# Hybrid attention encoder on one core: dilated products a step later, distance tables on two engines, value loads inside the blocks, four transposed pieces ahead of the layer barrier

## The chip, the cores and the metric

The kernel runs on one core of one Trainium2 chip. The time is device microseconds of one execution; a kernel is timed in several executions and the median is given. PE is the matrix engine (TensorE), DVE the vector engine, ACT the scalar engine, POOL GpSimd, and SP the engine whose queue issues the DMA transfers.

## The reference, cut to what matters

Two layers, a sequence of 1024 tokens, width 1024, everything in fp32. A layer projects the normalised input to queries, keys and values of three groups of heads, mixes each group in its own way, normalises, projects back and adds, and then does a SwiGLU feed-forward.

```
for l in range(DEPTH):                      # DEPTH = 2
    h = rms_norm(x, attn_norm[l])
    x = x + hybrid_mixer(h, ...)            # A: 2-D neighbourhood, 4 heads; B: +-128 tokens, 6 heads;
    h = rms_norm(x, ffn_norm[l])            # C: dilated windows, 6 heads
    x = x + swiglu(h, w_gu[l], w_down[l])

for window, d in ((128, 1), (512, 4), (2048, 16)):      # group C
    # every d-th token forms a sub-sequence of s // d tokens
    o, lse = banded_attention(to_sub(q), to_sub(k), to_sub(v), window // (2 * d), slopes, d)
# the three results are weighted by softmax(lse) over the branches and added
# banded_attention: sc = q @ k.T * hd**-0.5 - slope * distance * d, masked; softmax; @ v
```

## The kernel before

Everything is written out by hand: each engine has a program, and they meet at semaphores. A layer is one such set of programs, closed by a barrier of all engines. In a layer come the value projections, the query and key projections with their norms (units `UR`/`UH`/`UL`), the attention, the output projection, and the feed-forward (`RAW`, `WH`, `WL`, `OPH`, `ABH`, `ABL`), whose products are split into high and low fp32r parts.

The attention is a pipeline of steps k = 0 to 57 over 224 score tiles, four tiles to a step. A tile is one head of one block of 128 queries. The first 96 tiles (steps 0 to 23) are dilated: 16 groups of 6 heads, groups 0 to 7 of branch d=16 ("c3", 128 keys) and 8 to 15 of branch d=4 ("c2", 192 scores of 256 keys). From tile 96 on (step 24) follow eight token blocks of 16 tiles (6 of group B, 6 of branch d=1, 4 of group A), four steps each. In step k:

- PE computes the scores of tiles 4k to 4k+3 (line 2373, `psum<-KS,QS` or `psum<-QK`), then the weighted sums with the values of tiles 4k-8 to 4k-5 (`weigh`, line 2482, `psum<-VR,PT`), then transposes the probabilities of tiles 4k-4 to 4k-1 (line 2439, `psum<-ident,T`).
- DVE adds the distance table to the scores and takes the minimum (`tmin`, line 1659, `T<-TC,psum`), four tiles, and then copies the transposed probabilities from PSUM to `PT` (line 1830), up to step 12 all of them, later one of two pieces; ACT copies the other (line 1241).
- ACT takes the exponentials (line 1219), stores each finished group of sums to its buffer `G` (line 1212), and in steps 2 to 19 makes one distance table per step (`distance_table`, line 1151): the six of `TC2`, the six of `TC1`, the six of `TB`.
- POOL gathers the strided queries and keys of a dilated group into `QS` and `KS` (lines 2172 and 2173), one group per 1.5 steps, two buffers.
- SP's queue stores each dilated group to DRAM (`store_group`, lines 936 and 939; four `G` buffers, and `tmin` of group g waits until group g-4 is out), then loads the values of group g+4 to `VR` (`load_values`, lines 904 to 908), and from group 8 on also the bias tables and the values of the token blocks: nine loads to `VC` (line 952) and eight to `VA` (line 956). Behind all of them stands the load that brings the two dilated results back for token block 0 (line 986); DVE's `branch_min` (line 1746) in step 27 waits for it, `branch_min` of a later block for its own.

At the end of layer 0, PE transposes the first two of the sixteen pieces of the next layer's input (`turned`, line 2320, `psum<-ident,XN`) ahead of the barrier, and behind it multiplies piece 0 (`value_half(0, 0)`, line 2307, `psum<-VWH,HH`) and transposes pieces 2, 3 and 4 before it can go on with piece 1. Pieces 2 and 3 use banks whose last sums DVE adds to `X` just ahead (`add_last`, line 2098).

Of the kernel before, what the change touches and what calls it, by code (L numbers as in the profile page):

```python
# [22 lines left out]
def build_program(nc, x, gains, w_in, rpb, w_out, w_gu, w_down, out):  # L23
# [43 lines left out]
    with ctx:  # L67
# [96 lines left out]
        QS = sb("QS", [P, 2, 3, P], F32, "Q", 2048)  # L164

# [54 lines left out]
        WARM_START, WARM_LAYER = 72, 8  # L220
# [86 lines left out]
        for l in range(depth):  # L307
          with ExitStack() as layer:
# [38 lines left out]
            g_out_s = [sem(f"g_out{i}") for i in range(4)]  # L347
# [12 lines left out]
            dist_signed, dist_abs, dist_made = sem("dist_signed"), sem("dist_abs"), sem("dist_made")  # L360
            row_made, col_made, mask_made = sem("row_made"), sem("col_made"), sem("mask_made")
# [157 lines left out]
            order = []  # L519
            n_pt = 0  # L520
# [138 lines left out]

            def group_buf(bd, s):  # L660

                if bd["kind"] in ("c3", "c2"):
                    return G4[:, s // 6, :], s % 6
                return (GB[:, :], s) if s < 6 else (GC[:, 0, :], s - 6) if s < 12 else (GA, s - 12)
# [147 lines left out]
            def _(sp):  # L812
# [40 lines left out]
                sp.wait_ge(dist_made, 1)  # L853
# [76 lines left out]
                def store_group(gi):  # L930
                    sp.wait_ge(grp_s, gi + 1)
                    slot = gi % 4
                    if gi < 8:
                        g16 = g_dil[1].rearrange("(j r) c -> r j c", r=16)
                        for rr in range(2):
                            sp.dma_start(g16[2 * gi + rr], G4[64 * rr:64 * rr + 64, slot, :]).then_inc(g_out_s[slot], 16)
                    else:
                        g4 = g_dil[0].rearrange("(t p r) c -> r t p c", p=P, r=4)
                        sp.dma_start(g4[(gi - 8) // 2, gi % 2], G4[:, slot, :]).then_inc(g_out_s[slot], 16)

                for gi in range(4):
                    load_values(gi)

# [10 lines left out]
                def load_grid(c):  # L954

                    sp.dma_start(VA[ROWS * c:ROWS * c + ROWS, :, :, :].rearrange("p m h d -> p m (h d)"),
                                 v_a.rearrange("(r m c) d -> c r m d", m=MT, c=COLS)[c]).then_inc(va_in, 16)
# [3 lines left out]
                for gi in range(C_GROUPS):  # L961
# [18 lines left out]
                for slot in range(4):  # L980
                    sp.wait_ge(g_out_s[slot], 16 * 6)
# [1746 lines left out]
```

## Time and profile before

| | |
|---|---|
| median of 3 executions | 2338.93 us (2336.89 to 2340.94) |
| the profiled execution | 2340.14 us, of which its span is 2338.4 us |
| instructions | 40610 |
| PE busy | 2282.7 us |
| DVE, ACT, POOL busy | 1598.8, 1068.1 and 657.7 us |
| DMA | 225.34 MB, 96 GB/s on average |

A row of a view of instructions has the start in us from the span's start, the duration, engine, line, operation, output<-inputs, form and count; in brackets how long the engine had been idle before it, and what ended that. The lines are those of the kernel before; in the diff and the changed kernel they are a few higher.

### The profile page before, as it was taken

How to read it: one execution, taken by the hardware profiler on the slowest of the kernel's cores; microseconds unless marked ns; L12 is line 12 of the kernel's file. 1: busy time of each engine (PE TensorE's matmuls, PEld its weight loads, DVE VectorE, ACT ScalarE, POOL GpSimd, SP SyncE). 2: the span in 40 equal slices, each digit the busy share in tenths (PEclk: the TensorE clock that was granted, in tenths of full speed). 3: DMA queues.
4: the chain of work that ended last, by engine and by line, in shares of the span. 5: the costliest groups of instructions: out<-in, count | busy, mean ns of one | idle time of the engine just before them, and what ended most of it. 6: DMA issues, size and time to landing. Idle time of an engine off the chain costs nothing. (4 is left out here: it accounts for less than half of the span.)

```text
span 2338.4 us, 40610 instructions
## 1 busy us (share of the span) xinstructions
PE 2282.7 (98%) x15504; PEld 1889.8 (81%) x15504; DVE 1598.8 (68%) x2895; ACT 1068.1 (46%) x2048; POOL 657.7 (28%) x571
## 2 busy tenths in 40 slices
PE   9999889999999999999999998999999999999999
PEld 9988766787888888888899887667878888888887
DVE  5389879738555555789844897796475555557898
ACT  4333789735322222443443337896452223224434
POOL 1000456311444444100010005562124444440000
PEclk9999999999999999999999999999999999999999
DMA  7231341232222211721452314303322222218223
GB/s 249 66 53 53 95 119 31 101 124 70 81 82 90 82 55 55 291 82 54 137 175 58 56 45 117 105 28 123 104 72 82 81 81 83 62 45 315 68 81 104
DMA packets 234028, 225.34 MB, mean 96 GB/s; under 512 B 50292, under 2 KB 192116, under 8 KB 233848
## 3 DMA queue, kind: packets, MB, share of 16 engines
q1 hardware_dynamic: 233848, 222.89, 30.2%
q8 instruction: 119, 1.95, 0.3%
q14 instruction: 61, 0.50, 0.1%
HBM read 171.00 MB, written 53.41 MB: 96 GB/s over the span
## 5 line engine op out<-in xcount | busy, mean ns | idle before, releaser
L1925 DVE TENSOR_TENSOR WL<-RAW,WH 128x512 fp32r<-128x512 f32 x132 | 160.6, 1218 | 151.3 <-ACT WH L1374 151.3
L2677 PE MATMUL psum<-ABH 128*128 128x512 f32 x616 | 240.1, 390 | 1.1 <-DVE X L2008 1.1
L2678 PE MATMUL psum<-ABL,ABH 128*128 128x512 f32 x616 | 239.7, 389 | 0.0
L2679 PE MATMUL psum<-ABH,ABL 128*128 128x512 f32 x616 | 239.7, 389 | 0.0
L2643 PE MATMUL psum<-HL,WH 128*128 128x512 f32 x704 | 217.4, 390 | 0.7 <-DVE HL L1931 0.7
L2643 PE MATMUL psum<-OPH_t,WH 128*128 128x512 f32 x528 | 205.9, 390 | 3.5 <-DVE U L1946 3.5
L2643 PE MATMUL psum<-OPL_t,WH 128*128 128x512 f32 x528 | 205.7, 390 | 1.0 <-DVE OPH_t L1931 1.0
L1925 DVE TENSOR_TENSOR WL<-WS,WH 128x512 fp32r<-128x512 f32 x172 | 138.6, 807 | 84.2 <-ACT WH L1374 84.2
L2275 POOL TENSOR_TENSOR WS<-RAW 128x512 f32<-128x512 f32 x84 | 143.3, 1706 | 131.0 <-DMA x_res<-X 131.0
L2307 PE MATMUL psum<-HH,UH 128*128 128x512 f32 x448 | 174.5, 389 | 0.0
L2309 PE MATMUL psum<-HH,UL 128*128 128x512 f32 x448 | 174.3, 389 | 0.0
L2308 PE MATMUL psum<-HL,UH 128*128 128x512 f32 x448 | 174.3, 389 | 0.0
L1612 DVE RECIPROCAL RM<-RM 128x512 f32<-128x512 f32 x52 | 174.0, 3346 | 0.0
L1219 ACT ACTIVATE T<-T,G 128x192 f32<-128x192 f32 (+3 forms) x352 | 152.9, 470 | 17.1 <-DVE G L1659 15.7
L2643 PEld LDWEIGHTS psum<-HL,WH 128*128 128x128 f32 x704 | 131.7, 188 | 29.2 <-DVE HL L1931 1.5
L2172 POOL COPY QS<-QK 128x384 f32<-128x384 f32 x32 | 30.0, 937 | 438.4 <-DVE QK L1615 253.9
L2307 PE MATMUL psum<-PH,HH 128*128 128x512 f32 (+1 forms) x384 | 143.7, 374 | 0.0
L2309 PE MATMUL psum<-PH,HL 128*128 128x512 f32 (+1 forms) x384 | 142.6, 371 | 0.0
L2308 PE MATMUL psum<-PL,HH 128*128 128x512 f32 (+1 forms) x384 | 142.4, 371 | 0.0
L2643 PE MATMUL psum<-OPH_b,WH 128*128 128x512 f32 x352 | 137.3, 390 | 0.0
L2677 PEld LDWEIGHTS psum<-ABH 128*128 128x128 f32 x616 | 115.6, 188 | 26.5 <-DVE X L2008 2.0
L2643 PE MATMUL psum<-OPH_b,WL 128*128 128x512 f32 x352 | 137.0, 389 | 0.0
(270 smaller groups left out, 5526.2 us busy)
## 6 DMA issues: line engine op xcount, KB each, us to landing
RAW<-in_w_gu SPq DMA_DIRECT2D x176, 256.0 KB, 3.9
WDS<-in_w_down SPq DMA_DIRECT2D x88, 256.0 KB, 2.7
UR<-in_w_in SPq DMA_DIRECT2D x56, 256.0 KB, 3.3
g_mid<-GRES SPq DMA_DIRECT2D x28, 512.0 KB, 2.6
WDK<-in_w_down SPq DMA_DIRECT2D x44, 256.0 KB, 6.1
x_res<-X SPq DMA_DIRECT2D x2, 4096.0 KB, 13.3
PR<-in_w_out SPq DMA_DIRECT2D x32, 256.0 KB, 4.9
X<-x_res SPq DMA_DIRECT2D x2, 4096.0 KB, 13.7
```

Source lines behind the costliest of these rows:

```text
L1219: a.activation(T[:, t_slot(n), off:off + w], T[:, t_slot(n), off:off + w], ACT.Exp, scale=-1.0, bias=G[:, 6 * V1 + place_:6 * V1 + place_ ...
L1612: v.reciprocal(RM[:, hf, :], RM[:, hf, :]).then_inc(rec_s, 1)
L1925: v.tensor_tensor(WL[SLOT[i, j]][:, :, :], w_source(i, j), WH[SLOT[i, j]][:, :, :].bitcast(F32), ALU.subtract).then_inc(w_lo, 1)
L2172: g.tensor_copy(dst, dilated_rows(bd, T_CQ, q, P)).then_inc(staged, 1)
L2275: g.tensor_tensor(to[i][:, :, :], first, second, op).then_inc(w_sum, 1)
L2307: t.matmul(dst, sh, mh, start=start, stop=False)
L2308: t.matmul(dst, sh, ml, start=False, stop=False)
L2309: return t.matmul(dst, sl, mh, start=False, stop=stop)
L2643: last = t.matmul(dst[:, :], w[SLOT[i, j]][:, k, :], h[o][:, k, :], start=(i in (1, 5, 6) and k == 0 and part == 0), stop=(i in (2, 3, 4) ...
L2677: t.matmul(dst, ah, bh, start=open_, stop=False, skip_group_check=True)
L2678: t.matmul(dst, ah, bl, start=False, stop=False, skip_group_check=True)
L2679: last = t.matmul(dst, al, bh, start=False, stop=shut, skip_group_check=True)
```

## The change

Five edits, with their code below.

1. `weighed_at`: in the dilated steps the weighted sums are those of tiles 4k-12 to 4k-9, a step later than before. Step 25 does eight tiles, and from step 26 on all is as it was.
2. The dilated groups go round six buffers, not four: the four of `G4`, `GB`, and a new `GX`.
3. Of the 18 distance tables made in steps 2 to 19, ACT keeps those of steps 2, 4, 6, 8 and 10; DVE makes the other 13, behind its copies of the step.
4. Of the nine loads of `VC`, three stay among the dilated groups and six move between the token blocks; of each of the eight loads of `VA`, the half for blocks 0 to 3 stays and the half for blocks 4 to 7 moves behind the first load of the dilated results.
5. Four pieces, not two, are transposed ahead of the barrier, and four transposes of the identity follow them, whose result nothing reads.

Two pairs of setup semaphores are also merged into one each.

```diff
+            def weighed_at(k):
+                if k <= DILATED_STEPS:
+                    return range(max(4 * k - 12, 0), max(4 * k - 8, 0))
+                return range(4 * k - (12 if k == DILATED_STEPS + 1 else 8), 4 * k - 4)
...
+        G_DIL = [G4[:, 0, :], G4[:, 1, :], G4[:, 2, :], G4[:, 3, :], GB[:, :], GX[:, :]]
...
+            def group_slot(gi):
+                return gi % 6
+            def groups_out(slot, gi=C_GROUPS):
+                return sum(32 if before < 8 else 16 for before in range(slot, gi, 6))
...  # ACT, act_step
-                            if 2 <= k < 8:
+                            if k in (2, 4, 6):
                                 distance_table(TC2[:, k - 2, :], 384, 256, 4 * SLOPES[B_H + k - 2])
-                            elif 8 <= k < 14:
+                            elif k in (8, 10):
                                 distance_table(TC1[:, k - 8, :], 384, 256, SLOPES[B_H + k - 8])
-                            elif 14 <= k < 20:
-                                distance_table(TB[:, k - 14, :], 0, 384, SLOPES[B_ORDER[k - 14]])
...  # DVE, dve_step, behind copy_unit
+                def distance_table(tab, first, w, slope):
+                    v.tensor_scalar(tab, DIST[:, first:first + w], slope, None, ALU.mult).then_inc(table_s, 1)
+                    if k in (3, 5, 7):
+                        distance_table(TC2[:, k - 2, :], 384, 256, 4 * SLOPES[B_H + k - 2])
+                    elif k in (9, 11, 12, 13):
+                        distance_table(TC1[:, k - 8, :], 384, 256, SLOPES[B_H + k - 8])
+                    elif 14 <= k < 20:
+                        distance_table(TB[:, k - 14, :], 0, 384, SLOPES[B_ORDER[k - 14]])
...  # SP
-                        load_neighbours(2 * h)
-                        load_neighbours(2 * h + 1)
...
-                        if gi == C_GROUPS - COLS // 2:
-                            load_neighbours(MT)
-                        c = 2 * (gi - (C_GROUPS - COLS // 2))
-                        load_grid(c)
-                        load_grid(c + 1)
+                        m = gi - (C_GROUPS - COLS // 2)
+                        if m < NEAR_FIRST:
+                            load_neighbours(m)
+                        load_grid(2 * m, 0)
+                        load_grid(2 * m + 1, 0)
...
                 for b in range(MT):
...
                         sp.dma_start(GC[:, 1 + n, :], g_dil[n][b * P:b * P + P, :]).then_inc(g_back, 16)
+                    if b + NEAR_FIRST <= MT:
+                        sp.wait_ge(vc_in, 16 * (b + NEAR_FIRST))
+                        load_neighbours(b + NEAR_FIRST)
+                    if b == 0:
+                        sp.wait_ge(va_in, 16 * COLS)
+                        for c in range(COLS):
+                            load_grid(c, 1)
...  # PE, behind the barrier and ahead of it
-                    pe.sem_inc(xt_s, 2)
+                    pe.sem_inc(xt_s, 4)
...
-                for j in range(2 if l else 0, 4):
+                for j in range(4 if l else 0, 4):
                     turned(j)
...
-                    for j in range(2):
+                    for j in range(4):
+                        if j == 2:
+                            pe.wait_ge(last_added, 4)
                         turned(j)
+                    for i in range(WARM_LAYER):
+                        t.transpose(bank[2][:, P * i:P * i + P], ident[:, :], ident[:, :])
```

On PE the first weighted sums stand between the scores and the transposes of step 2. Before, from the scores of step 1 to those of step 3:

```order
L2431 MATMUL psum<-ident,T 128x128 x4
L2373 MATMUL psum<-KS,QS 128x128 x4
L2482 MATMUL psum<-VR,PT 64x65 x8
L2431 MATMUL psum<-ident,T 128x128 x4
L2373 MATMUL psum<-KS,QS 128x128 x4
L2482 MATMUL psum<-VR,PT 64x65 x8
L2439 MATMUL psum<-ident,T 128x64 x8
```

And now:

```order
L2464 MATMUL psum<-ident,T 128x128 x4
L2406 MATMUL psum<-KS,QS 128x128 x4
L2464 MATMUL psum<-ident,T 128x128 x4
L2406 MATMUL psum<-KS,QS 128x128 x4
L2516 MATMUL psum<-VR,PT 64x65 x8
L2472 MATMUL psum<-ident,T 128x64 x8
```

The order within a step (scores, sums, transposes) stays; one set of sums is gone from step 2. It comes back in step 25, where 16 rows of the last dilated sums become 32. Before, at steps 24 and 25:

```order
L2373 MATMUL psum<-QK 128x256 x4
L2482 MATMUL psum<-VR,PT 64x65 x16
L2439 MATMUL psum<-ident,T 128x64 x16
L2373 MATMUL psum<-QK 128x256 x2
L2373 MATMUL psum<-QK 128x192 x2
L2482 MATMUL psum<-VR,PT 64x65 x16
```

And now:

```order
L2406 MATMUL psum<-QK 128x256 x4
L2516 MATMUL psum<-VR,PT 64x65 x16
L2472 MATMUL psum<-ident,T 128x64 x16
L2406 MATMUL psum<-QK 128x256 x2
L2406 MATMUL psum<-QK 128x192 x2
L2516 MATMUL psum<-VR,PT 64x65 x32
```

On DVE a table stands between the copies of step 3 and the first `tmin` of step 4 (`ISA` is `tmin` and the reading of its minimum). Before:

```order
L1659 ISA G_96 128x1
L1830 COPY PT<-psum 128x256 x2
L1659 ISA T,G_96<-TC_89,psum 128x128
L1659 ISA G_96 128x1
L1659 ISA T,G_96<-TC_89,psum 128x128
```

And now:

```order
L1682 ISA G_96 128x1
L1853 COPY PT<-psum 128x256 x2
L1869 TENSOR_SCALAR TC_90<-DIST 128x256
L1682 ISA T,G_96<-TC_89,psum 128x128
L1682 ISA G_96 128x1
```

Whatever holds the table up holds up the next step's `tmin` too. On PE at the layer's end, before:

```order
L2679 MATMUL psum<-ABH,ABL 128x512
L2320 MATMUL psum<-ident,XN 128x128 x8
L2693 UNCONDITIONAL_BRANCH
L2301 UNCONDITIONAL_BRANCH
L2307 MATMUL psum<-VWH,HH 128x384
```

And now:

```order
L2712 MATMUL psum<-ABH,ABL 128x512
L2353 MATMUL psum<-ident,XN 128x128 x16
L2728 MATMUL psum<-ident 128x128 x4
L2730 UNCONDITIONAL_BRANCH
L2334 UNCONDITIONAL_BRANCH
L2340 MATMUL psum<-VWH,HH 128x384
```

Eight transposes moved ahead of the barrier (the first branch ends the layer's program), with four more behind them.

## Rows read from the trace of the kernel before

**Rows 1.** The page: busy time (share of the span) and instructions.

```profile
PE 2282.7 (98%) x15504; PEld 1889.8 (81%) x15504; DVE 1598.8 (68%) x2895; ACT 1068.1 (46%) x2048; POOL 657.7 (28%) x571
```

**Rows 2.** Busy time by stretch: us, then engines, clock share, DMA share, GB/s.

```profile
200.00:250.00 50.00, 50.00 (x222) 41.11 (x221) 45.91 (x31) 20.23 (x32) 0.00 (x0) 1.00 0.10 31
```

**Rows 3.** Timeline, one step of branch d=16 in layer 0.

```profile
263.45 0.71 PE L2482 MATMUL psum<-VR,PT 128*64 128x65 f32 x16 [0.39 <-DVE PT L1830]
264.10 0.46 PE L2439 MATMUL psum<-ident,T 64*128 64x64 f32 x8
264.59 0.76 DVE L1830 COPY PT<-psum 128x256 f32<-128x256 f32 x2 [0.41 <-PE psum L2439]
265.50 0.30 PE L2482 MATMUL psum<-VR,PT 128*64 128x65 f32 x3 [0.44 <-DVE PT L1830]
```

**Rows 4.** Busy by stretch (PE, PEld, DVE, ACT, POOL), dilated steps of both layers.

```profile
259.30:278.69 19.39, 15.29 (x289) 12.77 (x288) 14.26 (x92) 17.01 (x54) 15.10 (x16) 1.00 0.42 103
278.69:286.13 7.44, 6.65 (x128) 5.55 (x128) 5.42 (x29) 6.93 (x19) 4.97 (x5) 1.00 0.61 166
286.13:303.09 16.96, 14.32 (x282) 12.38 (x280) 9.02 (x46) 13.40 (x34) 9.24 (x8) 0.90 0.81 229
303.09:316.52 13.43, 12.53 (x278) 10.57 (x276) 9.20 (x47) 11.74 (x30) 8.40 (x11) 1.00 0.70 205
316.52:319.75 3.23, 2.70 (x56) 2.14 (x56) 2.01 (x11) 2.76 (x7) 3.15 (x4) 1.00 0.52 145
1423.84:1443.41 19.57, 16.15 (x304) 13.61 (x304) 14.36 (x92) 16.68 (x54) 15.84 (x16) 1.00 0.43 107
1443.41:1450.71 7.30, 6.28 (x115) 4.90 (x112) 5.34 (x28) 6.82 (x19) 4.23 (x4) 1.00 0.68 177
1450.71:1464.79 14.08, 12.51 (x282) 10.81 (x280) 9.11 (x47) 13.15 (x34) 9.25 (x8) 1.00 0.93 261
1464.79:1478.22 13.43, 12.53 (x278) 10.55 (x276) 9.20 (x47) 11.75 (x30) 7.18 (x9) 1.00 0.75 209
```

**Rows 5.** Timeline, the weighted sums of one step of branch d=4.

```profile
300.62 1.15 PE L2482 MATMUL psum<-VR,PT 128*64 128x65 f32 x32 [0.20 <-DVE PT L1830]
```

**Rows 6.** Timeline of PE, the longest stop in the dilated steps.

```profile
291.87 0.77 PE L2482 MATMUL psum<-VR,PT 128*64 128x65 f32 x18 [0.15 <-ACT PT L1241]
294.52 1.13 PE L2482 MATMUL psum<-VR,PT 128*64 128x65 f32 x14 [1.88 <-issue]
```

**Rows 7.** DVE operations by line: duration ns min/median/max, first and last start.

```profile
L1621 DVE TENSOR_TENSOR SQL<-SQ,SQH x56: 679/684/1326, 94.7 to 1418.8; 128x512 fp32r<-128x512 f32 x56
L1562 DVE TENSOR_SCALAR XN<-X,rstd x16: 746/753/756, 512.5 to 1698.8; 128x1024 f32<-128x1024 f32 x16
L1697 DVE TENSOR_SCALAR gvare<-gvar x48: 142/146/154, 332.6 to 1611.2; 128x1 f32<-128x1 f32 x48
```

**Rows 8.** SP's queue: timeline, then the loads of VR from issue to landing.

```profile
271.75 1.23 SPq L936 DMA_DIRECT2D g_d<-G  x2
273.03 1.24 SPq L904 DMA_DIRECT2D VR<-v_c  x2
...
DMA to landing us min/median/max: 2.3/2.7/5.6
```

**Rows 9.** Waits in step 27 of layer 1: us in total, times, longest.

```profile
DVE nmin L1746 <- DMA G<-g_d: 1.6, 1, 1.6
```

**Rows 10.** Timeline at the barrier between the layers.

```profile
1173.32 1.04 PE L2320 MATMUL psum<-ident,XN 128*128 128x128 f32 x8
1174.67 0.75 DVE L1542 SCALAR_TENSOR_TENSOR HL<-psum,GAINS,HH 128x512 fp32r<-128x512 f32 x1 [0.47 <-ACT HH L1111]
1177.56 0.41 PE L2307 MATMUL psum<-VWH,HH 128*128 128x384 f32 x1 [3.21 <-DVEq L1567]
1180.84 1.95 PE L2320 MATMUL psum<-ident,XN 128*128 128x128 f32 x12
1182.55 0.42 PE L2307 MATMUL psum<-VWH,HH 128*128 128x384 f32 x1
```

More of the change, by code:

```diff
@@ L346, in build_program @@
             vr_in = [sem(f"vr_in{i}") for i in range(4)]
-            g_out_s = [sem(f"g_out{i}") for i in range(4)]
+            g_out_s = [sem(f"g_out{i}") for i in range(6)]
             g_back = sem("g_back")
@@ L952, in load_neighbours, with load_grid @@
                     sp.dma_start(dst.rearrange("p h d -> p (h d)"), src).then_inc(vc_in, 16)
-                def load_grid(c):
-                    sp.dma_start(VA[ROWS * c:ROWS * c + ROWS, :, :, :].rearrange("p m h d -> p m (h d)"),
-                                 v_a.rearrange("(r m c) d -> c r m d", m=MT, c=COLS)[c]).then_inc(va_in, 16)
+                def load_grid(c, half):
+                    ms = slice(MT // 2 * half, MT // 2 * half + MT // 2)
+                    sp.dma_start(VA[ROWS * c:ROWS * c + ROWS, ms, :, :].rearrange("p m h d -> p m (h d)"),
+                                 v_a.rearrange("(r m c) d -> c r m d", m=MT, c=COLS)[c][:, ms, :]).then_inc(va_in, 16)
                 sp.wait_ge(va_out, 16)
@@ L1291, in act_step @@
                         if j == 2:
-                            if k >= 2:
-                                for n in range(4 * k - 8, 4 * k - 4):
-                                    if family_end(n):
-                                        store_result(n)
+                            for n in weighed_at(k):
+                                if family_end(n):
+                                    store_result(n)
                             for u in mine[:1]:
@@ L1652, in tmin @@
                     if place_ == 0 and dilated(bd):
-                        last_out = 32 * bd["i"] if k == "c3" else 64 + 16 * bd["i"]
-                        if last_out:
-                            dve.wait_ge(g_out_s[s // 6], last_out)
-                    if k == "b0" and s in (6, 12):
-                        dve.wait_ge(g_out_s[0 if s == 6 else 3], 96)
+                        gi = family(bd, s)
+                        if groups_out(group_slot(gi), gi):
+                            dve.wait_ge(g_out_s[group_slot(gi)], groups_out(group_slot(gi), gi))
+                    if k == "b0" and s in (0, 6, 12):
+                        slot = {0: 4, 6: 0, 12: 3}[s]
+                        dve.wait_ge(g_out_s[slot], groups_out(slot))
                     acc = G[:, 6 * V1 + place_:6 * V1 + place_ + 1]
@@ L2151, in _ @@
                 step(g.memset(D0[0:64, 704:768], BIGD))
-                g.memset(D0[64:128, 640:704], BIGD).then_inc(dist_made, 1)
-                pool.wait_ge(dist_made, 1)
+                g.memset(D0[64:128, 640:704], BIGD).then_inc(dist_pool, 1)
+                pool.wait_ge(dist_pool, 4)
                 pool.wait_ge(xt_s, 16)
@@ L2472, in weigh @@
                         if k == "b0" and s == 6:
-                            pe.wait_ge(vc_in, 16 * (MT + 1))
                             pe.wait_ge(v_ones, 5)
-                        if k == "b0" and s == 12:
-                            pe.wait_ge(va_in, 16 * COLS)
+                        if not dilated(bd) and s == 6:
+                            pe.wait_ge(vc_in, 16 * max(bd["i"] + 2, 3))
+                        if not dilated(bd) and s == 12 and bd["i"] in (0, MT // 2 - 1):
+                            pe.wait_ge(va_in, 16 * COLS * (2 if bd["i"] else 1))
                         if fam >= 2:
@@ L2522, in pe_step @@
                         pe.wait_ge(rmsq_s, 2 * QT - 1)
-                    if k >= 2:
-                        for n in range(4 * k - 8, 4 * k - 4):
-                            if n == 6:
-                                pe.wait_ge(rmsq_s, 2 * QT)
-                            weigh(n)
+                    for n in weighed_at(k):
+                        if n == 6:
+                            pe.wait_ge(rmsq_s, 2 * QT)
+                        weigh(n)
                     for i, u in enumerate(steps[k]):
```

36 lines of the change are left out of this document (19 added, 17 removed).

## Prediction

> **What bounds the kernel now.** I read the page first. PE is busy 2282.7 us of the 2338.4 us of the span, so all idle time of PE together is 55.7 us, and nothing in this change takes work from PE except by moving it [rows 1]. The views by stretch show where that idle time lies: in the projections PE is busy 50.00 of 50 us [rows 2], so nothing that happens there on other engines matters. In the dilated steps it is busy 15.29 of 19.39 us, then 12.5 of 13.4 us [rows 4]. Last I read the timeline of single steps, to see what ends PE's waits.
>
> Steps 3 to 11 (branch d=16) take 19.39 us in layer 0 and 19.57 us in layer 1 [rows 4], 2.16 us a step, and a timeline shows why [rows 3]: the transposes start at 264.10 and last 0.46, DVE copies from 264.59 for 0.76, PE, done with the next scores, waits 0.44 us and starts the weighted sums at 265.50, and these hold the next transposes back by 0.65. Sums to sums is 2.05 us. It is a ring of transposes, copy, sums, transposes, while no engine is full: PE 15.29/9 = 1.70 a step, DVE 14.26/9 = 1.58, ACT 17.01/9 = 1.89 [rows 4]. In branch d=4 PE works 2.50 us of a step of 2.69 (12.53 and 13.43 over five steps) [rows 4], and the rest is the same wait for a copy, 0.20 us [rows 5].
>
> On top lies one stop of 1.88 us in step 17 of layer 0 [rows 6], put down to nothing that waits on a semaphore, in a stretch in which DMA is 0.81 busy and the clock share is 0.90, against 1.00 around it [rows 4]: PE ran part of it at 1.2 instead of 2.4 GHz. Steps 15 to 19 take 16.96 us there and 14.08 in layer 1, where the clock stayed up.
>
> **The change part by part.** The sum is made against the profiled execution, 2340.14 us, which is 1.21 us above the median of 2338.93.
>
> *Sums a step later, steps 3 to 11.* The sums now read a copy made a whole step earlier, so the ring is broken; what is left is the fullest engine. DVE has 1.58 us a step, plus a table in five of the nine. The trace has no table on DVE. The same kind of instruction takes 0.146 us for one column and 0.753 for 1024 [rows 7]; on that line 256 columns are 0.30 and 384 are 0.37 us. It can also be held up by POOL, which is busy 15.10 of 19.39 us here [rows 4]: the low part of the squares, which reads two tensors of SBUF, takes 0.684 us in the median and 1.326 at most [rows 7], the long ones beside gathers of POOL. The least such hold is nothing, the most 0.64. I take half the gap, 0.32, because a copy of POOL is met at a chance point of it, in full share, since POOL is busy 78% and the table follows the copies at once. So DVE has 1.58 + 5/9 x (0.30 + 0.32) = 1.93. SP's queue allows about the same: a group of 1.5 steps needs two stores and two loads, 1.28 us from pair to pair [rows 8], 2.56 us a group or 1.71 a step, without the transfers of the variances. At 1.93, 18 steps take 34.7 us instead of 38.96: **-4.2**. Bounds: 1.75 a step (no hold, -7.5) and 2.05 (the ring's own length, hold in full, -2.1).
>
> *Steps 12 to 14.* Step 14 now has the short sums of branch d=16 (16 rows for 32, 0.71 us for 1.15 [rows 3, 5]); steps 12 and 13 lose the wait and get a table on DVE, which I set against each other. With 0.5 us less in each layer: **-1.0**.
>
> *Steps 15 to 19.* DVE has 9.02/5 = 1.80, a table of 0.37 and a hold of up to 0.64, mostly under PE's 2.50. I take 2.52 a step, 25.2 us for ten instead of 31.04 [rows 4]: **-5.8**. 3.3 of it is the stop and the half clock (16.96 - 5 x 2.69 is 3.5). They go if the stop came from crowded transfers: two of the three transfers that fill SP's queue behind each value load at that place, the two loads to VC, are gone from groups 8 to 11. Bounds: both stay (-2.5), and 2.50 a step (-6.0).
>
> *Steps 20 to 24.* No tables in either kernel; the wait of 0.2 goes: 10 steps at 2.50 for 26.86: **-1.9**.
>
> *Step 25.* It has sums of four more tiles, 1.08 us (a set of 32 rows takes 1.15 with its tail [rows 5]), of which half of its own idle time, 0.53 of 3.23 us [rows 4], may be filled. Two steps at 3.8 for 6.45: **+1.15**. This pays back what steps 2 and 14 lost.
>
> *Six buffers.* A `tmin` waited for a store of four groups before; with six it has three steps more. The long steps in 3 to 11 are mostly this and are in the first term.
>
> *Loads moved.* Nothing reads the moved loads before token block 2, eight steps after the first of them, which is their cover. Those ahead of the first load of the dilated results are fewer and half as large. DVE waits for it 1.6 us in step 27 of layer 1 [rows 9], and PE for DVE for a part of that; layer 0 has a shorter wait of the same kind. For both I take about half of one such wait: **-0.9**. Bounds: nothing and -1.6. What is queued behind SP's new waits for `vc_in` and `va_in` is the load for the next block, which is issued a block ahead of its reader.
>
> *Ahead of the barrier.* PE ends its eight transposes at 1174.36, is idle 3.21 us, starts the first products at 1177.56 and goes on with piece 1 at 1182.55 [rows 10], 4.99 us later for 12 products and 12 transposes. Twelve transposes more (1.56 us at 0.13 each, from 8 in 1.04) end at about 1175.9 instead; DVE arrives at 1175.42 [rows 10] and the barrier lets go 2.1 us after it, so the gap is covered but for up to 0.5. Behind it eight transposes of 0.16 are gone, 1.3 us, and more if the clock holds: the 12 transposes at 1180.84 take 1.95, where at full clock they would take 1.56, and the products ahead of them are stretched too. 0.8 at least, 2.4 at most; I take **-1.7**, as the idle stretch is halved.
>
> The Trainium skill (SBUF — State Buffer, section "SBUF: two separate sides") says that VectorE and GpSimd share one pair of ports, that the pair is an exclusive lock, and that a VectorE operation in a two-port mode waits for the whole GpSimd instruction and the other way round. The long squares in [rows 7] agree with such a lock. By that page each of the 26 tables waits for the rest of a gather; that would give the time of the first rival below.
>
> Sum: -4.2 - 1.0 - 5.8 - 1.9 + 1.15 - 0.9 - 1.7 = -14.35, so 2325.8 for the profiled execution and **2324.5** for the median.
>
> **The rivals.**
> *Tables held in full.* If every table costs DVE 0.30 to 0.37 plus 0.64 and the loss in one step is not won back in the next, steps 3 to 11 stay at 2.05 (-2.1), 12 to 14 gain 0.5, and 15 to 19 take 1.80 + 0.37 + 0.64 = 2.8 less what ACT and PE give back, 2.75 (-3.5). Sum: -2.1 - 0.5 - 3.5 - 1.9 + 1.15 - 2.6 = -9.4: 2329.5. For it: POOL's share of busy time. Against: it needs every table to meet a gather at its start.
> *The stop stays.* The 1.88 us are code or a queue, not the crowd of transfers, and the half clock follows: -14.35 + 3.3 = -11.0: 2327.9. For it: nothing in the row names a DMA. Against: layer 1 has the same code and no such stop.
> *PE alone bounds.* 1.75, 2.50, clock held at the barrier: -14.35 - 3.3 - 0.2 - 0.7 = -18.6: 2320.3. Against: DVE's 1.75 would have no slack at all.
> *The values come late (the other side).* Stores leave one step later, and each value load stands behind a store. SP is full from group 0 to 7. Group 7's values are issued at 273.03 to 274.27 and land 2.7 later [rows 8], at 277.0, and are read in step 12, which begins at 278.69 [rows 4] with 0.7 us of scores: 2.4 us to spare. Store and reader both move a step, but the nine steps between get 9 x 0.23 = 2.1 us shorter and the queue doesn't, so 0.3 is left. If they are late, PE stops, and each stop like that of [rows 6] costs the 3.3 us of above, 1.9 of them idle. From six such stops in the two layers the gain is gone and another 5 us lost; with all of groups 6 to 9 in both layers, eight stops, it is -14.35 + 26 = +12: 2351. Against: a late load delays everything equally and so restores its own lead.
> *Nothing comes of it.* Another ring (scores, `tmin`, exponential, transposes) is about as long as the one broken: 2.0 a step stays, and only the moved work and the barrier count. That gives -2 to -5: about 2335.
>
> **How the numbers follow.** Forecast 0.50, tables held 0.16, stop stays 0.12, PE alone 0.10, late values 0.04, nothing 0.08. The range of 2317 to 2332 leaves out the last two and half of their neighbours; the likeliest case alone is 2321 to 2328. About 0.2% (4.7 us) is what a measurement of this kernel tells from no change, so faster is below 2334.3: the first four cases, 0.88 less a little for the slow end of the second; same 0.09, slower 0.04.
>
> **What would show it.** Right: sums of steps 4 to 11 with no wait before them for `PT`, steps of 1.85 to 1.95, no stop over 1 us at step 17 and no clock drop there, DVE's minimum of block 0 without a wait, piece 1's products under 7 us behind the first transposes. Tables of DVE longer than 0.6 us would show the hold. Wrong: waits for `v_c` loads or long `issue` gaps at the sums, steps 3 to 11 still at 2.0 with another releaser, PE idle in step 25 or 27 for longer than before, a half-clock stretch in a new place.

## The result, and the profile after

The changed kernel takes 2341.02 us in the median of 20 executions (2336.0 to 2346.45), the kernel before 2338.6 us in 20 beside them (2334.09 to 2340.94). The ratio is 1.0015, 95% interval 1.0009 to 1.0022: two to five us slower, inside the 0.2% called no change or at its edge. I had forecast 2324.5, with 2317 to 2332 as the range and 0.87 for faster. That was wrong.

The profiled execution took 2338.12 us (span 2336.4), 2.0 below that of before: in one pair of executions the sign is the other way. The pair is not a fair one: the profiled execution of before lies 1.5 us above its median and had a mean granted clock of 0.996, that of the changed kernel lies 2.9 us below its median and had 0.998. The page, to be held against [rows 1]:

```profile
PE 2279.7 (98%) x15508; PEld 1886.1 (81%) x15508; DVE 1614.1 (69%) x2921; ACT 1058.2 (45%) x2022; POOL 659.9 (28%) x571
```

DVE has 15.3 us more work and ACT 9.9 less. The stretches that answer to [rows 4], by the view of busy time by stretch (PE, PEld, DVE, ACT, POOL, clock share, DMA share, GB/s), layer 0 and then layer 1, steps 2 to 11, 12 to 14, 15 to 19, 20 to 24, 25; the sixth line is step 27 of layer 0:

```profile
257.24:279.14 21.90, 17.80 (x324) 14.64 (x324) 19.23 (x106) 17.21 (x53) 17.61 (x18) 1.00 0.35 87
279.14:286.00 6.86, 5.83 (x102) 4.33 (x99) 6.30 (x31) 5.62 (x15) 4.27 (x4) 1.00 0.57 149
286.00:301.32 15.32, 13.60 (x305) 11.28 (x302) 12.35 (x51) 11.64 (x30) 9.42 (x9) 1.00 0.78 208
301.32:313.11 11.79, 11.60 (x258) 9.66 (x252) 9.09 (x46) 10.89 (x28) 7.35 (x9) 1.00 0.61 186
313.11:317.28 4.17, 3.64 (x88) 3.08 (x88) 2.01 (x11) 3.15 (x8) 4.01 (x6) 1.00 0.27 71
320.51:325.20 4.69, 3.42 (x58) 2.47 (x60) 2.37 (x13) 3.28 (x8) 0.00 (x0) 1.00 0.67 188
1417.07:1438.93 21.86, 17.75 (x324) 14.59 (x324) 19.21 (x105) 17.20 (x53) 17.55 (x18) 1.00 0.34 86
1445.79:1461.69 15.90, 13.88 (x279) 11.87 (x274) 11.09 (x51) 11.75 (x30) 9.42 (x8) 0.89 0.75 203
```

I cut every kernel in this way, a step from its first minimum on DVE to the next step's. Us, layer 0 / layer 1:

| steps | before | changed | forecast for both layers, change | measured |
|---|---|---|---|---|
| 2 to 11 | 21.49 / 21.68 | 21.91 / 21.86 | -4.2 | +0.6 |
| 12 to 14 | 7.45 / 7.30 | 6.86 / 6.86 | -1.0 | -1.0 |
| 15 to 19 | 16.96 / 14.08 | 15.32 / 15.90 | -5.8 | +0.2 |
| 20 to 24 | 13.43 / 13.43 | 11.79 / 12.46 | -1.9 | -2.6 |
| 25 | 3.23 / 3.23 | 4.17 / 4.17 | +1.15 | +1.9 |
| 27 | 4.01 / 4.53 | 4.69 / 6.14 | -0.9 | +2.3 |

These rows add up to +1.4, and with the 2.1 us at the barrier (below) to -0.7. The other 1.3 us by which the profiled execution is shorter lie where nothing was changed: there the kernel before ran longer at half clock, in two places (by stretch, kernel before),

```profile
430.00:445.00 15.00, 12.74 (x211) 10.15 (x207) 11.27 (x45) 8.75 (x21) 5.87 (x7) 0.77 0.34 100
1595.00:1605.00 10.00, 8.27 (x128) 6.48 (x126) 7.58 (x30) 7.19 (x18) 3.53 (x4) 0.83 0.39 127
```

where the changed kernel has 0.89 and 1.00.

**Where a table goes.** Timeline around the tables of steps 5 and 7, layer 0 (form as in [rows 3]):

```profile
265.38 1.40 POOL L2253 MEMSET VR<- 64x1560 f32 x1
265.39 1.52 DVE L1869 TENSOR_SCALAR TC<-DIST 128x256 f32<-128x256 f32 x1
266.84 0.27 DVE L1682 CUSTOM_DVE_ANT_0 T<-TC,psum 128x128 f32<-128x128 f32 x1
267.38 1.00 PE L2406 MATMUL psum<-KS,QS 64*128 64x128 f32 x8 [1.11 <-DVE GB L1682]
...
270.00 0.84 POOL L2205 COPY QS<-QK 128x384 f32<-128x384 f32 x1 [0.31 <-PE psum L2406]
270.10 0.89 DVE L1869 TENSOR_SCALAR TC<-DIST 128x256 f32<-128x256 f32 x1
```

The table of 256 columns that starts 0.01 us behind POOL's memset ends 0.13 behind its end; the next, started 0.10 behind a gather, ends 0.15 behind that. Between them the minimum is late, and PE stands still for 1.11 us because of it. All tables of DVE, by line (as [rows 7]):

```profile
L1869 DVE TENSOR_SCALAR TC<-DIST x14: 278/660/1524, 261.2 to 1443.0; 128x256 f32<-128x256 f32 x14
L1869 DVE TENSOR_SCALAR TB<-DIST x12: 344/351/1310, 285.7 to 1461.4; 128x384 f32<-128x384 f32 x12
```

A table of 256 columns takes 0.28 undisturbed (I had worked out 0.30), 0.66 in the median, 1.52 at most. The Trainium skill (SBUF — State Buffer, section "SBUF: two separate sides") has the shared pair locked for the whole of the other engine's instruction; the ends of these pairs agree with that. One case does not: the tables of step 9 take 0.28 us wherever DVE makes them, also where, by the profile, they run inside POOL's operation on `ROOTS` of 2.9 us (w1b_tables_ahead, 270.65 inside 270.19 to 273.12); the profile's spans on POOL are rough.

**A new stop.** POOL in layer 0 and layer 1, and PE behind it (timelines):

```profile
294.02 1.56 POOL L2226 TENSOR_TENSOR QK<-QK,RM_LAST 128x512 f32<-128x512 f32 x1 [3.76 <-DMA RM_LAST<-variances]
297.58 0.59 PE L2406 MATMUL psum<-KS,QS 64*128 64x192 f32 x4 [1.45 <-POOL KS L2206]
...
1453.54 1.57 POOL L2226 TENSOR_TENSOR QK<-QK,RM_LAST 128x512 f32<-128x512 f32 x1 [3.49 <-DMA RM_LAST<-variances]
1457.26 0.60 PE L2406 MATMUL psum<-KS,QS 64*128 64x192 f32 x4 [2.02 <-POOL KS L2206]
```

`RM_LAST` holds the roots of the last query tile, which POOL multiplies in (`scale_last`) between two gathers. SP spreads them with two transfers behind the store of group 7, and all stores now leave a step later. In the kernel before they were issued at 285.93 in layer 0 and POOL did not wait for them; in layer 1 it waited 1.1 us, and PE did not stop for it. Now they leave at 287.48, 1.55 us later, and POOL waits until 294.02, 3.1 us later than it went on before: part of the delay is in the transfers themselves, and why they take longer is not shown. The gather behind is late, PE stops, and in layer 1 half clock follows. By stretch:

```profile
1456.00:1462.00 6.00, 4.74 (x68) 4.17 (x70) 2.50 (x14) 2.69 (x6) 4.79 (x5) 0.72 0.57 174
```

**A longer wait.** DVE's wait for the dilated results of block 0 (as [rows 9]), layer 0 and layer 1:

```profile
DVE nmin L1769 <- DMA G<-g_d: 1.7, 1, 1.7
...
DVE nmin L1769 <- DMA G<-g_d: 3.2, 1, 3.2
```

**The barrier** came out better than forecast (timeline, answers to [rows 10]):

```profile
1170.76 2.04 PE L2353 MATMUL psum<-ident,XN 128*128 128x128 f32 x16
1175.35 0.41 PE L2340 MATMUL psum<-VWH,HH 128*128 128x384 f32 x1 [2.11 <-DVEq L1589]
1177.88 0.42 PE L2340 MATMUL psum<-VWH,HH 128*128 128x384 f32 x1
```

From the first transposes to piece 1's products it is 7.12 us, against 9.23 before, with no half clock. The clock is part of this, as experiment 2 shows.

**Why the medians differ more than the profiles.** Each execution lists its mean granted clock. At equal share the changed kernel is 1.6 us slower at 0.998 (2338.6, 5 executions, against 2337.0 of 41 of the kernel before, from all its executions beside the experiments) and 2.1 at 0.997 (2340.4 against 2338.3), and it has a low share more often: 7 of its 20 are at 0.995 or 0.996, with medians of 2346.0 and 2343.5, against 8 of 97. So single profiles place a stop, but a gain of 2 us is only to be read from the medians.

### The profile page after: what moved, and what is told of

Its sections match the earlier page's. It is cut to its first block and busy times, and to the rows that moved or that the text cites. A ratio compares the mean times of both kernels' runs of the same rounds, so it can differ in the third digit from the quotient of the medians.

```text
span 2336.4 us, 40648 instructions
## 1 busy us (share of the span) xinstructions
PE 2279.7 (98%) x15508; PEld 1886.1 (81%) x15508; DVE 1614.1 (69%) x2921; ACT 1058.2 (45%) x2022; POOL 659.9 (28%) x571
## 3 DMA queue, kind: packets, MB, share of 16 engines
q8 instruction: 119, 1.95, 0.3%
## 5 line engine op out<-in xcount | busy, mean ns | idle before, releaser
L1244 ACT ACTIVATE T<-T,G 128x192 f32<-128x192 f32 (+3 forms) x304 | 132.6, 477 | 21.8 <-DVE G L1682 20.8
L2676 PE MATMUL psum<-OPL_b,WH 128*128 128x512 f32 x352 | 137.0, 389 | 0.0
```

Source lines behind the costliest of these rows:

```text
L1244: a.activation(T[:, t_slot(n), off:off + w], T[:, t_slot(n), off:off + w], ACT.Exp, scale=-1.0, bias=G[:, 6 * V1 + place_:6 * V1 + place_ ...
L2676: last = t.matmul(dst[:, :], w[SLOT[i, j]][:, k, :], h[o][:, k, :], start=(i in (1, 5, 6) and k == 0 and part == 0), stop=(i in (2, 3, 4) ...
```

## The experiments

Every kernel below has its own runs of the kernel before on the same chip, and the ratio is against those.

**1. All tables back on ACT; and, apart from it, the roots a group earlier.**

```diff
# x1_tables_act: the changed kernel with edit 3 undone
# x2_root_early: the changed kernel with
-            SPREAD_AT = {0: 0, 1: 1, 6: 2, 7: 3}
+            SPREAD_AT = {0: 0, 1: 1, 5: 2, 6: 3}
```

> The changed kernel with all 18 distance tables back on ACT; the other four edits stay. Theory 1 (POOL holds the tables): in the changed kernel the tables of DVE in steps 3 to 11 lasted 0.66, 1.52, 0.89, 0.28 and 0.85 us, each long one ending with the instruction of POOL beside it, and the next minimum waits behind them. Without them steps 2 to 11 should fall from 21.9 us to about 19.5 to 20 in each layer, 4 us in all, and the time to about 2336 to 2337. Rival (another ring of scores, minimum, exponential and transposes has the same length): steps 2 to 11 stay at 21 to 21.9 us and the time does not move by more than 1 us. The stop before the scores at step 18 or 19 comes from POOL waiting for its DMA and should stay at 1.3 to 2.0 us under either.

> The changed kernel with the two transfers that spread the last query rows' roots issued one group earlier (behind the stores of groups 5 and 6 in place of 6 and 7). Theory 2 (the roots come late): in the changed kernel POOL waits 3.8 and 3.5 us for RM_LAST before it scales the last tile, its gather of keys ends late, and PE stops 1.45 us in layer 0 and 2.02 us in layer 1, followed there by 3.4 us at half clock. With the transfers 2.7 us earlier most of POOL's wait goes, both stops fall under 0.3 us, and the profiled time by 3.5 to 5 us, to 2333 to 2335; the median by 3 to 6, as the runs scatter less. Rival (POOL is late because DVE's tables hold its gathers): POOL's wait for the DMA goes, but the stops stay over 1 us and the time stays at 2338 to 2341.

| | steps 2 to 11 | 15 to 19 | 27 | median, ratio |
|---|---|---|---|---|
| x1_tables_act | 18.82 / 18.82 | 15.04 / 17.57 | 4.85 / 6.24 | 2337.15, 1.0005 [0.9994, 1.0016] |
| x2_root_early | 21.89 / 21.88 | 12.97 / 13.26 | 4.95 / 4.58 | 2337.43, 1.0001 [0.9992, 1.001] |

Both mechanisms are there. Without tables on DVE steps 2 to 11 fall by 3.1 us in each layer (x1, by stretch):

```profile
257.50:276.32 18.82, 15.93 (x300) 13.42 (x300) 15.68 (x101) 18.43 (x58) 16.10 (x17) 1.00 0.34 86
```

But of the 6.1 us little is left: with the steps shorter, POOL waits longer for the same roots (3.90 and 5.42 us, for 3.76 and 3.49), and PE's stop behind it grows from 1.45 and 2.02 to 2.06 and 3.54 us. With the roots earlier that stop is gone in both layers, so DVE's tables were not what made POOL late. The time missed what was expected of x2 all the same (2337.4 for 2333 to 2335): steps 15 to 19 are 5.0 us shorter, steps 20 to 24 give 1.9 of it back (12.59 and 13.52 us for 11.79 and 12.46, with a stop of 1.04 us in layer 1), and the half clock at the barrier, which the profiled changed kernel does not have, costs some 1.6. Against its own runs of the kernel before, each remedy alone brings 2 to 3 us: the change's loss, and no more.

**2. The barrier alone, and the split of the tables alone.** The kernel before with edit 5, and with edit 3.

> The kernel before with only the four transposes ahead of the barrier and the four of the identity behind them. Piece 1's products came 2.5 us after piece 0's in the changed kernel, 5.0 in the one before, and there was no half clock. If the edit does this by itself: 3.5 to 4.4 us faster, 2334.5 to 2335. If the clock of the changed kernel stayed up for another reason (a busier stretch ahead of it): 0.8 to 1.7 us, 2337 to 2338.

> The kernel before with only the split of the tables: ACT keeps five, DVE makes thirteen. Theory 1: each table on DVE costs 0.3 to 1.5 us ahead of the next minimum, and in the kernel before the ring of transposes, copy and sums is on the path, so steps 3 to 11 grow by half of it, 1 to 1.5 us a layer, steps 15 to 19 by 0 to 1: 2340 to 2343. Rival (DVE has the time: 1.58 of 2.16 us a step): 2338 to 2339.

x3_barrier_only: 2335.11 us, 0.9996 [0.9987, 1.0004]. The medians say 2.2 us less, the interval does not leave out no change. At equal share it is not faster (2335.1 at 0.999, where the kernel before has 2334.6); it only has the high shares more often, 10 of 11 executions at 0.998 or above against 60 of 97. Its profiled execution, 2332.0 us of span, keeps full clock wherever PE has work, over the barrier too (by stretch, and x4_split_only, which does not have the edit):

```profile
1170.00:1185.00 15.00, 12.89 (x85) 12.22 (x84) 11.96 (x20) 8.94 (x17) 6.09 (x11) 1.00 0.40 140
1170.00:1185.00 15.00, 11.48 (x74) 10.79 (x73) 10.96 (x18) 8.02 (x16) 5.35 (x11) 1.00 0.23 63
```

In profiled x1 and x2 the clock fell there in spite of the edit (share 0.83 in 1170 to 1180), and in x4 it stayed up without it: the edit does not decide the clock. The traces part the two. From the first of the transposes ahead of the barrier to step 2 of layer 1 the kernel before takes 248.4 us and x4, at full clock, 247.1; with the edit it is 246.3 us at full clock (changed kernel, x3) and 247.9 with one half clock at the barrier (x1, x2). So the edit itself is worth 0.8 us, and the other 1.3 of the 2.1 are the clock. x4_split_only: 2340.9 us, 1.0017 [1.0008, 1.0025], steps 2 to 11 at 22.25 / 22.39. The split alone costs as much as the whole change did.

**3. Both remedies, and from there one edit at a time.** y1_act_root is the changed kernel with both. y2_g_back, y3_no_lag, y4_dummy and z1_loads_back change it further:

```diff
# y2_g_back (SP), block 0's two loads; for block 0 the branches exchange buffers
                 for gi in range(C_GROUPS):
                     store_group(gi)
+                    if gi == 14:
+                        for slot in range(6):
+                            sp.wait_ge(g_out_s[slot], groups_out(slot, 14 if slot == 1 else 8))
+                        load_back(0, 1)
+                    elif gi == 15:
+                        for slot, last in ((2, 15), (4, 11), (0, 13)):
+                            sp.wait_ge(g_out_s[slot], groups_out(slot, last))
+                        load_back(0, 0)
# y3_no_lag
+                return range(max(4 * k - 8, 0), max(4 * k - 4, 0))
# y4_dummy (DVE, ahead of the last copy of steps 3, 5, 7, 9, 11)
+                                v.tensor_copy(TB[:, k // 2, 0:256], bank[u["bank"]][:, 0:256])
# z1_loads_back: edit 4 undone
```

> The changed kernel with all tables back on ACT and the two transfers of the roots one group earlier, so both remedies of the two runs before at once. If each does what it did alone (steps 2 to 11 at 18.8 us a layer; no stop over 0.3 us at step 18 or 19), steps 2 to 26 take 18.8 + 6.7 + 12.9 + 12.5 + 4.2 + 3.3 = 58.4 us a layer, 8 to 9 us less in all than in the changed kernel, and the time is 2331 to 2333. Rival: the faster POOL and SP lose it again, in a stop of POOL for the roots (its steps come 3 us sooner) or in step 27, where DVE waited 3.2 us for the load of the dilated results: 2335 to 2337.

> The same as y1_act_root, and the two loads of the dilated results for token block 0 leave earlier: that of branch d=16 behind the store of group 14, that of branch d=4 as soon as groups 8, 10, 12 and 14 are out (block 0 needs no odd group), ahead of the last two loads of the grid values. Theory 3 (step 27 waits for this load alone: 4.7 to 6.2 us against 3.8 with no wait): step 27 falls to 3.8 to 4.2 us in both layers, 2 to 3 us less than y1_act_root. Rival (the wait is crowding of the transfers, which stays): step 27 stays above 4.6 us and the time within 1 us of y1_act_root.

> y1_act_root with the weighted sums two steps behind the scores again, as in the kernel before; six buffers, loads and barrier as changed. If the lag is what took steps 2 to 11 from 21.5 to 18.8 us: they go back to 20.5 to 21.5, steps 20 to 24 to 13.4, step 25 to 3.2; 5 to 7 us slower than y1_act_root. If six buffers did it: steps 2 to 11 stay under 19.5 and the time is that of y1_act_root or 1 us below.

> y1_act_root with one more copy of 256 columns out of PSUM on DVE in steps 3, 5, 7, 9 and 11, where the changed kernel had its tables; its result is written over later and read by nothing. It costs DVE about 0.38 us each, more than an undisturbed table (0.28), but reads PSUM, so it should not wait for POOL. Theory 1 in its narrow form (the hold by POOL is what hurts): steps 2 to 11 stay within 0.7 us of y1_act_root's 18.8. Rival (DVE has no time for any fifth operation ahead of the next minimum): steps 2 to 11 grow by 1.5 to 3 us a layer.

> y1_act_root with the value loads of the token blocks where they were before (all nine of VC and all eight whole ones of VA among the dilated groups). The kernel before, and its two variants with those loads in place, stopped 1.3 to 1.9 us at the weighted sums of step 17 or 18 in layer 0, put down to nothing; no kernel with the loads moved did so by more than 0.8. Theory 4 (crowded transfers made that stop): it comes back with over 1.2 us, steps 15 to 19 of layer 0 go from 13.7 to 15 or more, and the time is 1 to 3 us above y1_act_root. Second question, step 27: 4.4 and 6.0 us in y1_act_root, 4.0 and 4.5 in the kernel before. If the moved loads, eight of which leave right behind the load of the dilated results, crowd it, step 27 falls by 0.5 to 1.5 us with them back; if the wait only grew because the steps ahead are shorter, it stays or grows.

| | 2 to 11 | 15 to 19 | 20 to 24 | 26 and 27 | median, ratio |
|---|---|---|---|---|---|
| y1_act_root | 19.02 / 18.81 | 13.72 / 12.89 | 12.70 / 12.46 | 7.62 / 9.80 | 2328.74, 0.9961 [0.9947, 0.9974] |
| y2_g_back | 18.82 / 18.88 | 13.63 / 12.68 | 12.37 / 12.65 | 6.67 / 7.57 | 2325.55, 0.9949 [0.9936, 0.9963] |
| y3_no_lag | 20.61 / 20.66 | 14.48 / 13.57 | 13.49 / 13.70 | 6.96 / 7.26 | 2332.89, 0.9978 [0.9969, 0.9987] |
| y4_dummy | 19.63 / 20.01 | 13.44 / 12.70 | 12.69 / 12.52 | 8.41 / 10.79 | 2331.76, 0.9973 [0.9962, 0.9984] |
| z1_loads_back | 19.00 / 18.77 | 14.26 / 13.86 | 12.99 / 12.38 | 8.43 / 10.96 | 2334.21, 0.9991 [0.998, 1.0002] |

Together the two remedies bring about 12 us by the medians, though each alone brought 2 to 3. That x1 ran into the wait for the roots is shown; no such wait is to be found for x2, whose 5.0 us of gain in steps 15 to 19 went as told above, in part to the clock. The profiles are of little help here, as that of y1 is its slowest execution (2334.35 us, share 0.996). The lag is worth 4.1 us (y3 less y1): it takes steps 2 to 11 from 20.6 to 18.9. What takes them from 21.6 to 20.6 a layer is not separated: six buffers and moved loads are two candidates, but z4_before_g_back below, which has neither, shows 20.75 in layer 1. The moved loads are worth 5 to 7 (z1 against y1, by medians and by ratios; z1's executions scatter by 15 us, and half of them are at shares of 0.995 and 0.996); in z1's trace two stops with no releaser are back, though steps 15 to 19 of layer 0 are at 14.26, not at the 15 expected, and the profiles of steps 2 to 54 account for only 2.3 us.

y4 lies between its two theories. Its extra operation on DVE is never held (0.41 us in each of its ten uses) and costs 0.6 and 1.2 us in five of them; five tables, which occupy DVE for 4.2 us with their holds, cost 3.1. So an operation at that place costs something without any hold, a fifth to two fifths of the tables' cost. Its uses (layer 1):

```profile
L1895 DVE COPY TB<-psum x5: 411/412/414, 1418.7 to 1434.0; 128x256 f32<-128x256 f32 x5
```

y2 is as expected, and shows one wait behind the one removed (timeline, layer 1):

```profile
1469.77 0.42 DVE L1698 CUSTOM_DVE_ANT_0 T<-TA,psum 128x256 f32<-128x256 f32 x1 [1.36 <-DMA g_d<-G]
1471.12 0.17 DVE L1785 TENSOR_TENSOR nmin<-G 128x6 f32<-128x6 f32 x1 [0.24 <-DMA G<-g_d]
```

Group A's heads of block 0 write the buffer that the last dilated group fills.

**4. Order round the buffers, roots earlier still, catching up in step 24; and block 0's loads in the kernel before.**

```diff
# z3_ring: y2_g_back with
-                return gi % 6
+                return (0, 1, 2, 5, 4, 3)[gi % 6]
# z2_all: z3_ring with SPREAD_AT = {0: 0, 1: 1, 4: 2, 5: 3} and, as w2b_ring_24,
-                if k <= DILATED_STEPS:
+                if k < DILATED_STEPS:
# z4_before_g_back: the kernel before with y2's loads
```

> y2_g_back with another order round the six buffers, 0, 1, 2, 5, 4, 3 in place of 0 to 5: the last group then fills GX, which nothing else needs, and not the buffer that group A's heads of block 0 write first. In y2_g_back DVE waited 1.4 us in layer 1 for the store of the last group ahead of the first minimum of step 27. That wait should be gone: steps 26 and 27 together from 7.57 to 6.7 us in layer 1, unchanged (6.67) in layer 0: 0 to 1 us faster than y2_g_back.

> z3_ring with the transfers of the roots one more group earlier, and the four late sums caught up in step 24 in place of 25. POOL waited 2.4 us for the roots in layer 0 of y2_g_back and PE stopped 0.6 us; that should go. Steps 24 and 25 exchange 0.9 us, which leaves the sum of them the same; the store of group 14 leaves a step sooner. 0 to 1.5 us faster than z3_ring.

> The kernel before with only the earlier loads of the dilated results for block 0. DVE waited 1.1 and 1.6 us for them in step 27, which took 4.0 and 4.5 us; 3.4 is what it took in y2_g_back. 1 to 2 us faster than the kernel before if the wait is on the path, nothing if DVE's time there is covered by PE's own work.

> z3_ring with the four late sums caught up in step 24 in place of 25, and the roots left where z3_ring has them. z2_all, which also had the roots a group earlier, took 14.9 and 14.6 us for steps 15 to 19 against 13.6 and 13.2, with a stop of 1.95 us in layer 1. If the still earlier roots did that: steps 15 to 19 back at 13.2 to 13.7, steps 25 to 27 at 3.2, 3.2 and 3.4, and 2323 to 2326. If the catching up did it or it was chance: 2326 to 2328.

z3_ring: 2326.7 us, 0.9958 [0.9945, 0.9971]; steps 26 and 27 at 6.76 / 6.92, the wait gone, the time not better than y2's. z2_all: 2327.16 us, 0.9959 [0.9946, 0.9971], steps 15 to 19 at 14.86 / 14.58. w2b_ring_24: 2325.83 us, 0.9953 [0.9939, 0.9967], 15 to 19 back at 13.71 / 12.75, as expected if the still earlier roots did it, in one profile of each; the 0.9 us of step 25 stand in steps 20 to 24 now (13.62 / 14.11). These three and y2 cannot be told apart by time. z4_before_g_back: 2335.42 us, 0.9991 [0.9982, 1.0], step 27 at 3.44 / 3.44. So a wait of 1.1 and 1.6 us stood in the kernel before too, and going round it takes 1.7 us from step 27 and about 2 from the median, whose interval just reaches no change.

**5. The tables of DVE ahead of its copies.** x2_root_early with the thirteen tables moved up; then only the six of `TB` on DVE, ahead of the copies, in z3_ring.

```diff
+                    if k in (3, 5, 7): ...        # the tables, then
                     for u in steps[k]:
                         if u["engine"] == 0:
                             copy_unit(u)
-                    if k in (3, 5, 7): ...
```

> x2_root_early (tables split over both engines, roots one group earlier) with the thirteen tables of DVE ahead of its copies of the step, where it waits for PE's transposes, in place of behind them, where the next minimum waits for it. If the place is what made them dear: steps 2 to 11 fall from 21.9 us to 18.5 to 19.5 in each layer and the time to 2328 to 2331. If the hold by POOL is what made them dear wherever they stand: steps 2 to 11 stay at 20.5 us or more, with single tables still over 0.6 us, and the time stays at 2334 to 2338.

> z3_ring with only the six tables TB (steps 14 to 19) on DVE, ahead of its copies; the other twelve stay on ACT. With all thirteen ahead of the copies steps 15 to 19 took 12.1 and 12.3 us, against 13.6 and 13.2 in z3_ring, while in steps 2 to 14 the split gained nothing. So steps 15 to 19 should fall by 2 us in the two layers and the rest stay: 2323.5 to 2325.5. If those short steps came from the split in steps 2 to 13 too (a better lead of DVE or POOL), they stay at 13.2 to 13.6, and the time at 2326 to 2327.

w1b_tables_ahead: 2330.46 us, 0.9972 [0.9963, 0.9982], 6 to 7 us better than x2_root_early, each against its own runs of the kernel before. Tables in layer 1 (steps 15 to 19 with 14, then steps 3 to 11, each first in x2_root_early and then here), and stretches (steps 2 to 11 of both layers, 15 to 19 of both):

```profile
L1869 DVE TENSOR_SCALAR TB<-DIST x6: 344/731/1250, 1446.3 to 1459.6; 128x384 f32<-128x384 f32 x6
L1869 DVE TENSOR_SCALAR TB<-DIST x6: 351/908/1361, 1438.5 to 1450.8; 128x384 f32<-128x384 f32 x6
L1869 DVE TENSOR_SCALAR TC<-DIST x5: 284/832/1507, 1421.9 to 1438.9; 128x256 f32<-128x256 f32 x5
L1869 DVE TENSOR_SCALAR TC<-DIST x5: 283/290/729, 1416.3 to 1432.0; 128x256 f32<-128x256 f32 x5
```

```profile
257.04:278.37 21.33, 16.90 (x316) 14.15 (x316) 17.88 (x105) 17.37 (x53) 17.65 (x18) 1.00 0.35 89
1413.98:1433.00 19.02, 16.30 (x301) 13.66 (x300) 16.97 (x105) 17.25 (x53) 16.28 (x17) 1.00 0.33 85
285.20:297.33 12.13, 12.13 (x272) 10.41 (x267) 12.13 (x51) 10.72 (x28) 9.74 (x9) 1.00 0.86 244
1439.98:1452.24 12.26, 12.14 (x275) 10.38 (x273) 12.26 (x52) 10.97 (x29) 9.13 (x8) 1.00 0.86 240
```

The six `TB` tables are held as long as ever (0.91 us in the median), and it costs nothing: in steps 15 to 19 PE is busy 12.13 of 12.13 us, with v1 the best of all kernels here. With the tables behind the copies and held about as much (x2) these steps took 12.97 and 13.26 us, so the place is worth 0.8 to 1.0 us a layer there. In steps 3 to 11 two things changed at once: moved up, the tables mostly miss POOL's instructions, and the five of layer 1 last 1.95 us together, for 4.2 behind the copies. So the fall from 21.88 to 19.02 us does not tell the place from the hold. That a hold delays the next minimum is seen at 265.39, that the place costs without a hold is seen in y4; how the 3.1 us divide between them is not shown. In layer 0 steps 2 to 11 stayed at 21.33, outside the 18.5 to 19.5 expected, with one stop of 1.98 us behind a late store of ACT, which I did not explain.

v1_tb_ahead: 2326.18 us, 0.996 [0.9947, 0.9974]; steps 15 to 19 at 12.16 / 12.28 as expected, but 12 to 14 at 6.99 / 7.02 for 6.43 / 6.45 and step 27 at 4.14 / 4.09 for 3.53 / 3.41, where the shorter steps meet block 0's load again. The 2.4 us were given back, and the time missed the 2323.5 to 2325.5 expected.

The lowest medians here, y2_g_back with 2325.55 and w2b_ring_24 with 2325.83, are 11 to 12 us under the kernel before, and 13 to 15 under the changed one.

## Why the prediction was wrong, point by point

- **Sums a step later, steps 3 to 11.** The ring was right and broken: with the tables back on ACT steps 2 to 11 take 18.8 us, 1.88 a step. The price of the tables was wrong, and this is the first step of the prediction that failed (-4.2 forecast, +0.6 measured). I took 0.30 and a hold of 0.32 as DVE time that is averaged over the steps (1.93 a step). But the table stood last in the step, ahead of the next minimum, and so a held one was on the path at once: minimum, then the scores that wait for it (PE idle 1.11 us at 267.38). A mean over the steps says nothing about that; that the next minimum stands behind the table was there to see in the order of DVE's instructions. The size was off too: the five tables take 4.2 us in a layer, 0.84 each, where I had 0.62. My rival of tables held in full took 2.05 a step, the length of the broken ring, as its worst; measured 2.19. The rival "nothing comes of it" had the ring of scores, minimum, exponential and transposes, and 2.0 a step; it was nearest, at 0.08.
- **Steps 12 to 14.** -1.0, as forecast.
- **Steps 15 to 19.** The stop of [rows 6] went, as I had said it would with fewer transfers, and z1_loads_back brought such stops back (1.38 and 1.02 us). This term failed by the most, +0.2 for -5.8. What I missed, a term put at nothing, is that the lag moves every store on SP, and with the stores the roots that hang on them: 1.45 and 2.02 us of stop and a half clock in a new place. I had followed the value loads behind the stores and not the transfers of `SPREAD_AT`. Without this the term was -5.8 forecast and -4.8 measured (x2: 26.23 for 31.04).
- **Steps 20 to 24.** -1.9 forecast, -2.6 measured.
- **Step 25.** +1.15 forecast, +1.9 measured: the double set takes 2.09 us in one piece, and nothing filled step 25's own idle time.
- **Loads moved.** -0.9 forecast for step 27, +2.3 measured. The load of the dilated results left 1.15 us sooner (319.81 for 320.96), but step 26 began 2.5 us sooner: the double sums come ahead of the last group's. The wait is set by that store and load, not by what was moved: with the loads back it is longer still (z1). I named the releaser rightly and left out that every gain ahead of it lengthens it.
- **Barrier.** -1.7 forecast, -2.1 measured in the profile, 2.2 by the medians of x3. That the number came out is luck: 0.8 of it is the edit, the lower bound of my term, and 1.3 is a half clock that did not fall there in this execution and did in x1 and x2.

Late values, the rival on the other side, did not come: no wait for `VR` ends one of the long stops in the changed kernel. They begin to show in the faster ones: such a wait ends a stop of 0.89 us in y1_act_root (273.30) and one of 1.13 in w2b_ring_24 (1437.32).

What stays open: the one stop of w1b in layer 0; how the cost of the tables divides between hold and place; why the transfers of the roots took longer; and how far the scatter of the executions, 10 us in the changed kernel, comes from where half clock falls. That was read from shares, not tested.

## What to carry to other kernels

An operation moved to an engine with idle time is priced by what stands behind it in the step, not by the engine's mean load: five tables behind the copies, in front of the next minimum, cost 3 us a layer, and six held ones ahead of the copies, where DVE waits anyway, cost nothing. A lag on one queue moves everything issued behind it, so list every transfer of that queue and its reader's time, the rare ones above all. And where a stage ends in a wait for a fixed chain of transfers, shortening the steps ahead pays only after that chain is moved: 6.1 us of shorter steps brought 2 to 3 while POOL still waited for the roots, and two remedies of 2 to 3 us each brought about 12 together.

## What the runs showed of the hardware

The stops "<-issue" have a common mark. Code comes over the DMA engines too; the packets meant here are those of 16 KB on queue 8, which carries nothing else (119 in the kernel before). In the kernel before there is none of them between 284.8 and 291.9, and one starts within 292.00 to 292.04; in z1_loads_back none between 282 and 288.9, and one within 288.90 to 288.95. PE goes on 2.5 and 2.25 us later. The DMA view of the kernel before, 291.9 to 292.3 us, and PE in z1 (timeline):

```profile
q1 hardware_dynamic: 105, 0.15, 103.3%
q8 instruction: 1, 0.02, 17.4%
```

```profile
291.17 0.75 PE L2396 MATMUL psum<-KS,QS 64*128 64x192 f32 x5 [1.38 <-issue]
```

The data queue fills all 16 engines at that moment. Of the twelve such stops over 0.8 us in the dilated steps of all profiled kernels, ten end 2.2 to 2.7 us after the start of such a packet, one 2.9 and one 6.9. The packet alone is not enough, as most are followed by no stop: in the same steps of these kernels there are some 280 of them. That PE stood still for its code, and that crowding makes code late, fits most of them and would explain what edit 4 bought; no run here changed the code's transfers themselves, so it is argued and not shown.
